# First weights of four stages of a hybrid encoder layer loaded in the stage ahead

## The reference, cut to what matters

```
h    = rms_norm(x) * (1 + scale(c)) + shift(c)
proj = h @ w_in                        # split among three branches and the merge gates
yA   = rwkv7(proj parts, states)       # delta-rule state, 8 heads of 64
yB   = latent attention(cq, ckv, kr)   # low-rank q and kv, 8 heads, softmax, chunk mask
yC   = stick_breaking(sq, sk, sv)      # 8 heads of 64
merged = sum over branches of sigmoid(gate) * ((y * silu(z)) @ w_branch)
x    = x + gate(c) * (merged @ w_out)
```

## Time and profile before

| | us |
|---|---|
| median of 3 runs | 5002.68 |
| the runs | 5002.68, 4989.94, 5006.99 |
| profiled execution, time | 4988.4 |
| profiled execution, span | 4986.7 |
| PE busy in it | 4462.7 |
| mean granted clock | 0.958 |

### The profile page before, as it was taken

The page is one execution under the profiler, slowest core; times in us unless marked ns, Lnnn a source line. Parts: engine busy times, 40 slices in busy tenths (PEclk is TensorE's granted clock), DMA queues, the critical chain, the costliest instruction groups (busy, mean ns, idle before and its releaser), DMA issues. The chain is left out here.

```text
span 4986.7 us, 75926 instructions
## 1 busy us (share of the span) xinstructions
PE 4462.7 (89%) x29584; PEld 3065.1 (61%) x29584; DVE 2222.8 (45%) x4666; ACT 1620.2 (32%) x3854; POOL 715.8 (14%) x938
## 2 busy tenths in 40 slices
PE   6898898878989989999969998887799899899999
PEld 2556656556756667777425566565567566577774
DVE  2355655245534463434223556551455344625342
ACT  2333333345533341212023332233355333412110
POOL 0010010000000005543000100100000000155430
PEclk9999999999999999999989999998999999999999
DMA  5000110210011103232240101102100121132322
GB/s 212 26 12 26 29 15 16 86 48 20 16 53 65 63 24 128 93 106 77 76 170 26 14 25 29 17 21 80 50 18 16 51 77 55 35 120 85 112 80 68
DMA packets 150452, 291.40 MB, mean 58 GB/s; under 512 B 53268, under 2 KB 79124, under 8 KB 144742
## 3 DMA queue, kind: packets, MB, share of 16 engines
q1 hardware_dynamic: 149976, 281.75, 17.8%
q10 hardware_dynamic: 112, 4.72, 0.3%
HBM read 239.08 MB, written 52.06 MB: 58 GB/s over the span
## 5 line engine op out<-in xcount | busy, mean ns | idle before, releaser
L1010 PE MATMUL banks<-hT,w_piece 128*128 128x384 f32 x1536 | 557.7, 506 | 2.3 <-ACT raw L1114 2.1
L2179 PE MATMUL banks<-hT,w_piece 128*128 128x384 f32 x1152 | 389.4, 493 | 17.4 <-DMA w_piece<-in_w_cols 16.0
L1010 PEld LDWEIGHTS banks<-hT,w_piece 128*128 128x128 f32 x1536 | 286.0, 197 | 175.4 <-issue 21.9
L2179 PEld LDWEIGHTS banks<-hT,w_piece 128*128 128x128 f32 x1152 | 216.5, 192 | 171.8 <-issue 20.5
L2468 PE MATMUL banks<-hT,w_gate 128*128 128x288 f32 x1152 | 301.0, 412 | 17.6 <-DMA w_gate<-in_w_cols 17.6
L2468 PEld LDWEIGHTS banks<-hT,w_gate 128*128 128x128 f32 x1152 | 223.0, 194 | 80.3 <-DMA w_gate<-in_w_cols 18.2
L2525 PE MATMUL banks<-hT,mergedT 128*128 128x512 f32 x576 | 247.5, 593 | 0.0
L1952 DVE SCALAR_TENSOR_TENSOR keysT<-banks,gains,rstd 64x128 f32<-64x128 f32 (+1 forms) x272 | 112.0, 412 | 260.8 <-ACT rstd L1866 258.3
L2571 DVE TENSOR_TENSOR gate_quarters<-gate_kept,banks 128x288 f32<-128x288 f32 x144 | 65.4, 454 | 329.9 <-PE banks L2468 326.9
L2534 ACT ACTIVATE gate_kept<-banks 128x288 f32<-128x288 f32 x144 | 59.1, 410 | 456.9 <-PE banks L2468 456.9
L2468 PE MATMUL banks<-h_sums,w_gate_sums 128*128 128x288 f32 x768 | 194.2, 407 | 0.1
(11 more groups left out here) (362 smaller groups left out, 9087.8 us busy)
## 6 DMA issues: line engine op xcount, KB each, us to landing
w_gate<-in_w_cols SPq DMA_DIRECT2D x96, 512.0 KB, 4.3
w_piece<-in_w_cols SPq DMA_DIRECT2D x68, 512.0 KB, 4.6
w_ada<-in_w_ada SPq DMA_DIRECT2D x12, 2048.0 KB, 10.4
w_branch<-in_w_br SPq DMA_DIRECT2D x96, 256.0 KB, 2.8
y_branch<-y_gated SPq DMA_DIRECT2D x12, 1152.0 KB
sb_cached_keysT<-in_sbkT SPq DMA_DIRECT2D x8, 1024.0 KB, 6.7
sb_cached_values<-in_sbv SPq DMA_DIRECT2D x8, 1024.0 KB, 5.2
hT<-in_w_out SPq DMA_DIRECT2D x4, 2048.0 KB, 10.3
```

The lines of the kernel that those rows point to most:

```text
L1010: last = mm(dst, w[0 if kind in ("k", "v") else 1][:, k, :], hT[:, k, c], start=(k == 0), stop=(k == KD - 1))
L2179: last = mm(ps[:, bank[n], 0:TG], w[wn % 3][:, k, :], hT[:, k, TG * g:TG * g + TG], start=(k == 0), stop=(k == KD - 1))
```

## The change

A tile `ahead` [128, 1344] is allocated for the whole kernel. The rwkv tile `lora` becomes its first 1152 columns. Four times in a layer, weights go into it or into another tile that outlives the stage:

1. In the last rwkv fused stage SP's first DMA brings w_latent's k = 0, 1 into `ahead`. The latent stage loads the other six k in three parts of two, each with a semaphore; PE's first row tile goes k by k over both column halves.
2. In latent, behind the nine stores of ckv, SP loads w_ukv and w_uq of head pair 0 of pairs into `ahead`. In pairs the gains have a semaphore of their own and are issued first.
3. In pairs, ahead of the weights of head pair 2, SP loads piece q of head pair 0 of stick-breaking into `ahead`. There the load of piece 3 (z of head pair 0) no longer waits for a fill.
4. In stick-breaking SP loads the gate weights of merge's unit 0 into a tile that spans both stages, and POOL makes their sums there, ahead of all its gate work. Merge starts without either.

Besides, in merge `h_sums` counts twice for each half (after the second and the fourth sum), PE waits for them apart, and `h_sum(1)` moves from ahead of the branch additions of unit 11 to behind the fifth addition.

```diff
+        ahead = sbt("weights_ahead", [P, 2 * (QL + KVL + RP)])
...
-        lora = ctx.enter_context(nc.sbuf_tensor("lora", [P, T], F32))
+        lora = ahead[:, 0:T]
...   rwkv_fused, SP
+            else:
+                sp.dma_start(ahead[:, :].rearrange("p (k n) -> p k n", k=2), A["w_lat"][l, :, 0:2]).then_inc(ahead_loaded, 16)
...   latent, SP
-                sp.dma_start(w[:, 0:KD // 2, :], A["w_lat"][l, :, 0:KD // 2]).then_inc(wa_loaded, 16)
-                sp.dma_start(w[:, KD // 2:KD, :], A["w_lat"][l, :, KD // 2:KD]).then_inc(wb_loaded, 16)
+                for q, loaded_q in enumerate((wa_loaded, wb_loaded, wc_loaded)):
+                    sp.dma_start(w[:, 2 * q:2 * q + 2, :], A["w_lat"][l, :, 2 * q + 2:2 * q + 4]).then_inc(loaded_q, 16)
...
+                sp.dma_start(ahead[:, 0:4 * P].rearrange("p (k n) -> p k n", k=2), A["w_ukv"][l, 0]).then_inc(ahead_loaded, 16)
+                sp.dma_start(ahead[:, 4 * P:7 * P].rearrange("p (k n) -> p k n", k=3), A["w_uq"][l, 0, :, :, 0:P]).then_inc(ahead_loaded, 16)
...   latent, PE
-                pe.wait_ge(wa_loaded, 16)
...
+                    halves = ((0, 0, QL), (1, QL, NL))
+                    for b, a, e, k in [(*half, k) for k in range(KD) for half in halves] if i == 0 else [(*half, k) for half in halves for k in range(KD)]:
+                        if i == 0 and b == 0 and k >= 2 and k % 2 == 0:
+                            pe.wait_ge((wa_loaded, wb_loaded, wc_loaded)[k // 2 - 1], 16)
...   latent_pairs, SP
+                if h == 2:
+                    sp.dma_start(ahead[:, 0:KD * P].rearrange("p (k n) -> p k n", k=KD), A["w_cols"][l, G_SQ]).then_inc(ahead_loaded, 16)
...
-            weights(0)
-            sp.dma_start(par[:, :], A["lat_par"][l]).then_inc(once_loaded, 16)
+            sp.dma_start(par[:, :], A["lat_par"][l]).then_inc(par_loaded, 16)
...   stick_breaking, SP and POOL
-            for kind in "qkv":
+            for kind in "kv":
                 load(kind, 0)
...
             load("k", 1)
+            for q in range(2):
+                sp.dma_start(wg0[:, q, :, :], A["w_cols"][l, G_GATE + q]).then_inc(wg_loaded, 16)
...
             by_sequence(0)
+            pool.wait_ge(wg_loaded, 32)
+            quarter_sums(nc.gpsimd, InOrder(pool, wg_sums), wg0, wgs0, KD // 2)
...   merge, PE
-                pe.wait_ge(wg_loaded[u % 2], 32 * (u // 2 + 1))
                 if u >= 1:
+                    pe.wait_ge(wg_loaded[u % 2], 32 * ((u + 1) // 2))
                     pe.wait_ge(tanh_done, 4 * u)
...
-                pe.wait_ge(gate_sums, u + 1)
-                pe.wait_ge(h_sums, tp + 1)
+                if u >= 1:
+                    pe.wait_ge(gate_sums, u)
+                pe.wait_ge(h_sums, 2 * tp + 1)
...
                 pe.wait_ge(kept, 6 * u + 2)
+                pe.wait_ge(h_sums, 2 * tp + 2)
...   merge, DVE
-                if u == NU // 2 - 1:
-                    dve.wait_ge(products, 14 * u + 7)
-                    h_sum(1)
                 add(u, 9, 4, bq[:, 0, :], bk[:, 0, :], 4)
...
                 add(u, 12, 6, bq[:, 1, :], bk[:, 2, :], 3)
+                if u == NU // 2 - 1:
+                    h_sum(1)
```

More of the change, by code:

```diff
@@ L177, in build @@
             modulation(nc, S, A, l, ps, con, gates, (x_prompt, x_sample, x_copied), hT)
[L178 to L181, removed]
+            rwkv(nc, S, A, O, l, ps, con, hT, yg, zg, ahead)
+            latent_attention(nc, S, A, O, l, ps, con, hT, yg, zg, q_rope, ahead)
+            with nc.sbuf_tensor("w_gate_ahead", [P, 2, KD, P], F32) as wg0, nc.sbuf_tensor("w_gate_sums_ahead", [P, 3, KD // 2, P], F32) as wgs0:
+                stick_breaking(nc, S, A, O, l, ps, con, hT, yg, ahead, wg0, wgs0)
+                merge(nc, S, A, l, ps, con, hT, yg, gates, x_tile, wg0, wgs0)
 def modulation(nc, S, A, l, ps, con, gates, x_state, hT):
@@ L1401, in _ @@
                         pe.wait_ge(copied, i - 1)
[L1402 to L1406, removed]
+                    halves = ((0, 0, QL), (1, QL, NL))
+                    for b, a, e, k in [(*half, k) for k in range(KD) for half in halves] if i == 0 else [(*half, k) for half in halves for k in range(KD)]:
+                        if i == 0 and b == 0 and k >= 2 and k % 2 == 0:
+                            pe.wait_ge((wa_loaded, wb_loaded, wc_loaded)[k // 2 - 1], 16)
+                        wk = w01[:, k, a:e] if k < 2 else w[:, k - 2, a:e]
+                        last = mm(ps[:, 2 * (i % 2) + b, 0:e - a], hT[:, k, P * i:P * i + P], wk, start=(k == 0), stop=(k == KD - 1))
                     last.then_inc(projected, 1)
@@ L1599, in latent_pairs @@
              "y0_stored", "y1_stored", "y2_stored", "vec")
-    with S.stage(*names) as (block, sb, (once_loaded, w0_loaded, w1_loaded, qa_loaded, qb_loaded, gate0_loaded, gate1_loaded,
+    with S.stage(*names) as (block, sb, (once_loaded, par_loaded, ahead_loaded, w0_loaded, w1_loaded, qa_loaded, qb_loaded, gate0_loaded, gate1_loaded,
                                          fill_ready, free0, free1, free2, free3, free6, free7, squared, summed, rooted, spread, zeroed,
@@ L1721, in begin @@
                 kind, h, p, step = fills[n]
-                if kind == "norm" and p == LA_PREP[0] or n == 0:
-                    pe.wait_ge(w_loaded[h % 2], 32 * (h // 2 + 1))
+                if kind == "norm" and p == LA_PREP[0] and h >= 1:
+                    pe.wait_ge(w_loaded[h % 2], 32 * ((h + 1) // 2))
                 if uses[n] >= 1:
@@ L2038, in stick_breaking @@
         w = [sb(f"w_piece{i}", [P, KD, P]) for i in range(3)]
+        w_of = [ahead[:, 0:KD * P].rearrange("p (k n) -> p k n", k=KD)] + [w[n % 3] for n in range(1, len(pieces))]
         Q = [sb(f"sb_queriesT{i}", [P, T]) for i in range(2)]
@@ L2356, with quarter_sums, merge @@
 TQ = T // 4
-def merge(nc, S, A, l, ps, con, hT, yg, gates, x_tile):
+def quarter_sums(eng, own, w, s, half, sem=None):
+    a11, a12, a21, a22 = (w[:, i, half * j:half * j + half, :] for i in range(2) for j in range(2))
+    own(eng.tensor_tensor(s[:, 0], a21, a22, ALU.add))
+    own(eng.tensor_tensor(s[:, 1], s[:, 0], a11, ALU.subtract))
+    own(eng.tensor_tensor(a21, a11, a21, ALU.subtract))
+    own(eng.tensor_tensor(s[:, 2], a12, s[:, 1], ALU.subtract), sem)
+def merge(nc, S, A, l, ps, con, hT, yg, gates, x_tile, wg0, wgs0):
     V, mm = nc.vector, nc.tensor.matmul
@@ L2403, in _ @@
                     sp.wait_ge(products, 14 * (u - 2) + 7)
-                for q in range(2):
+                for q in range(2 if u else 0):
                     sp.dma_start(wg[u % 2][:, q, :, :], A["w_cols"][l, G_GATE + KD * b + 2 * m + q]).then_inc(wg_loaded[u % 2], 16)
```

85 lines of the change are left out of this document (44 added, 41 removed).

## The result

The changed kernel takes 4971.24 us (median of 8 runs, 4962.36 to 4983.36), the kernel before in the same session 5004.49 (8 runs, 4988.59 to 5011.93). The ratio is 0.9947, with an interval of 0.9934 to 0.9960. By the ratio it is faster by 26.5 us, 0.53% (20 to 33 us by the interval); the two medians themselves lie 33.3 us apart. The prediction was 43.5 us. The direction, the four starts and the median's place inside the range of 4937 to 4977 held; the gain was forecast 1.6 times too large by the ratio, 1.3 times by the medians. That the median lies inside the range says little for the sum behind it: two of its terms failed, and the width of the range covered that.

A forecast was written before the change was run, and what follows sets the result against it. PE, with work in 89% of the span, was taken to bound the kernel. Starts 40.1 plus h_sum 4.4 less POOL 1.0 gave 43.5 us, so 5002.7 - 43.5 = 4959 us; range for 8 in 10: 4937 to 4977.

The forecast's parts named there:

- the four starts: Starts of latent, pairs, stick-breaking, merge: PE begins with SP's first issue, gaining 11.8, 10.1, 8.3 and 9.9 us, sum 40.1.
- Rival 3: At the starts: PE starts as late as before, the barrier setting it; only h_sum's gain left, 4999 us; chance 0.04.
- POOL in stick-breaking: Gate sums on POOL block DVE's operations: 0.5 us lost in a layer, bounds 0 and 2, together 1.0.
- The next due times: Behind the four starts: later weights, first squares and norms, pieces and y sums come in time; a latent miss costs at most 1 us.
- h_sum: Merge, units 11 and 12: moving the second half's sums gains 2.2 us a layer despite POOL's blocking, together 4.4, bounds 1 and 10.
- The clock: Behind each start the low stretch stays as it is; bound 1.5 us either way at each of eight starts, 4 us overall.
- a stage ends less than 3 us earlier than its start gained: Test for the stages: if this happens, or a hidden load releases PE, ACT or DVE, the prediction is wrong.
- Rival 4: At the starts: slower, thinner PE work keeps the clock at 1.2 GHz; time 5023 us at 20 us low each; chance 0.03.
- Rival 2: Starts half given back through waits in latent, pairs and merge: 20 of 40 us stay, time 4979; chance 0.10.

The follow-up runs named there:

- the run with latent's late start: Changed kernel with PE held at latent's start until the weights k = 2, 3 have landed; timed once at 4993.5 us.
- the timed run with POOL's wait: Changed kernel with POOL's sums of unit 13 held until DVE's second addition of unit 12; median 4959.98 us of 6 runs, ratio 0.9931 to before.

## Why the prediction was right and wrong

**The starts: right.** All four starts came within 0.1 us of the barrier, with the barrier as releaser, and no moved load became a releaser of PE. In pairs the stage gained 5.5 and 5.6 us for 5.1 forecast, in stick-breaking 3.8 and 5.4 for 3.7 and 4.6, less 0.5. In merge the start alone, with `h_sum(1)` in its old place, gave 5.4 and 5.0 for 4.95. Rival 3 is refuted.

**POOL in stick-breaking: the blocking seen, its price not.** DVE's busy time in the stage rose by 1.3 and 2.5 us. But the stages gained 3.8 and 5.4, what their starts gained or more. Nothing is seen of the 0.5 us in a layer; zero was inside its bounds of 0 to 2.

**The next due times: right.** PE meets no wait for a DMA inside latent's first tile, ACT's and DVE's first work in pairs waits for nothing new, and the y sums in merge stall nobody. They begin 9.0 us behind the barrier, not at the "some 6 us" of the prediction.

**h_sum: the mechanism right, the term mis-sized, and the sign wrong (10 us of the 17).** Forecast +4.4 for both layers. Measured -5.8 in the changed kernel (against the run with the old place), and -3.8 on the kernel before. Three numbers of that step failed. First, the queue behind the four gate sums: POOL's four branch weight sums come next on its list and block DVE too. Of the eight short operations counted at 0.49 us, three took 0.87, and from the end of the sums (2119.49) to the end of unit 12's first addition (2124.71) it is 5.2 us instead of 3.9. The three blocked sums of 3.1 us were right: the four took 3.5 longer than at 1.36. So the third copy ended 13.9 us behind unit 12's start instead of 12.5, and the stall was 3.73 instead of 2.8. Second, the clock: "no gap of under 3.25 us has shown the lower clock here" was a hope for a gap that turned out longer than the old one. Third, the price of the clock was read from one stretch of 3.4 us, and the new one lasted 6.8 (3.4 in the run with latent's late start). The stated lower bound of 1 us for `h_sum`, "0.5 of gain is left", assumed both at their best. A bound below zero was called for: two waits of nearly equal length (3.25 against 2.8) with a cost of blocking known only from one pair of operations.

**The clock: the step that failed in latent (10 us of the 17).** "I take the low stretch as it is" looked at the starts alone, and there it held roughly: in latent 5.8 us of work at the low clock in the changed kernel, which costs 1.3 us more than before, and in merge 0.8. (The test "back at 1.00 within 5 us of each start" failed in latent.) What was left out is that an earlier start also moves every later gap of the stage. Latent has one of 4.0 us some 90 us behind its start, at the turn of the last row tile. Before, it was followed by 6.9 us at 1.2 GHz, after by 13.6. The prediction read the clock for merge's unit 11 and for the starts, and never for latent's gap, although a window on the trace of before would have shown it. The two failed steps account for 20 us. Pairs and stick-breaking gave 3 more than forecast, which leaves the 17 that are missing. Rival 4 said that the clock could take the gain back, but through thin work at the starts; the place was wrong. Rival 2 came near the size by luck (24 us, against 26.5 by the ratio): it had other mechanisms, and none of those happened: no second part of weights, no norm and no y sum was late.

Of its own tests, "a stage ends less than 3 us earlier than its start gained" was met in latent (start 6.1 us, stage 1.0) and in merge (start 5.1, stage 2.0 and 2.6). It found the two steps that had failed.

What stays open is why the gap brings 13.6 us of low clock when it begins 89.9 us behind the barrier, and 6.8 to 6.9 when it begins 94 to 95 us behind it. The runs show only that it does, in both layers of every kernel that starts early (but the one with the gap filled) and of every kernel that starts late.

## What to carry to other kernels

Time saved at a stage's start must be followed through every later idle gap of that stage to its end: read the granted clock behind each gap before, and allow for twice the low stretch after, as latent and merge of the changed kernel showed. Before work is moved on DVE, list all that POOL has queued for that time, to the end of its list and not only the first group, and price each DVE operation beside it at POOL's time plus its own. Where two placements each end in a wait of about 3 us, neither is a gain; holding POOL back or filling the gap with work that PE has anyway (here 7 and 5 us in a layer) is.

## What the runs showed of the hardware

**DVE and POOL slow each other down in turn.** With a queue on both, a sum of 128x1152 on DVE goes from 1.36 to 2.31 us and one of 128x512 on POOL from 1.27 to 2.26. A DVE operation with one input from the banks wasn't held: it took 0.46 us beside POOL. The Trainium skill ("SBUF — State Buffer", section "SBUF: two separate sides") has the shared port pair as an exclusive lock for the whole instruction. By that rule two engines that both have work would alternate and each operation would show nearly the sum of both. From 1.36 and 1.27 us that is an estimate of 2.6; the trace comes near it, with 2.3.

**The same gap, two lengths of low clock.** A gap of 4.0 us in latent was followed by 6.8 to 6.9 us at the low clock in the kernels that start late, and by 13.6 in those that start early. A stall of 3.24 us in merge was followed by none (623.99 us) or 3.4 us (625.03) in the two layers of one run. A stall of 3.72 to 3.73 was followed by 6.8 in the changed kernel and in the kernel before with the new place, and by 3.4 in the run with latent's late start.

**Stages with two lengths.** One fused stage (the second pair of heads) has two lengths in one execution of the kernel before, 115.5 in layer 0 and 122.6 in layer 1, and differs in the granted clock alone:

```profile
462.36:577.88 115.52, 100.73 (x381) 58.86 (x381) 63.95 (x125) 33.93 (x76) 16.74 (x17) 0.97 0.13 18
2940.22:3062.84 122.62, 107.92 (x381) 62.23 (x381) 63.90 (x125) 33.94 (x76) 16.72 (x17) 0.90 0.14 16
```

Pairs does the like (with early starts 376.8 to 378.2, or 383.7 to 385.1 us). In the changed kernel the fused stage took 122.6 and 122.5 us, and 115.8 in layer 0 of the timed run with POOL's wait, so both lengths occur with early starts as well. Two or three such stages that flip from run to run would make about the spread of 20 us and more among a kernel's runs; that is an estimate from the eight profiled executions, and why a single run could not tell the 6 us of an experiment. The Trainium skill ("TensorE: Matmul & The Clock Gate", section "Part 1: The HAM clock gate (the "warmup" mystery)") says of a kernel's start that the number of matmuls at the low clock varies from run to run in the same kernel. These stages, in the middle of a kernel, vary likewise; latent doesn't: its stretch had the same length to 0.1 us in every layer and kernel of one kind.
